# Block two's head units cut into five pieces, and every piece, search round and turn placed anew

## The reference

```
h = rms_norm(x, attn_norm_g);  proj = h @ w_in            # 1024 -> 3656 columns
mq, mk, mv, dq, dk, dv, sq, sk, sv, iq, ik, iw = split(proj)
qk(t) = rope(rms_norm(t per head of 64))                  # for mq, mk, dq, dk, sq, sk; iq and ik: rope alone
moba  = softmax(mq mk^T / 8, causal) mv                   # 4 heads
diff  = (softmax(q1 k1^T / 8) - lam * softmax(q2 k2^T / 8)) dv, then rms_norm per head   # 4 heads
score = sum over 8 heads of iw_h * relu(iq_h ik^T / 8);  keep the 64 highest keys of each query
dsa   = softmax(sq sk^T / 8 over the kept keys) sv        # 4 heads
x = x + concat(moba, diff, dsa) @ w_out
h2 = rms_norm(x, ffn_norm_g);  x = x + (silu(h2 @ w_gate) * (h2 @ w_up)) @ w_down
```

## Time and profile before

| | |
|---|---|
| median of three runs | 1726.27 us |
| profiled execution, its own time | 1728.09 us |
| its span, first to last instruction | 1726.3 us |
| mean granted TensorE clock | 0.973 |
| TensorE busy | 1611.4 us, 93% |
| VectorE busy | 1048.4 us, 61% |
| ScalarE busy | 768.1 us, 44% |
| DMA | 322.41 MB, mean 187 GB/s |

### The profile page before, as it was taken

How to read it: one execution, slowest core, us unless ns; L and a number is a source line. 1 busy time by engine, 2 the same in 40 slices (tenths; PEclk the granted TensorE clock), 3 DMA queues, 4 the chain that set the end, 5 groups by cost and what they waited for, 6 DMA issues and landing times.

```text
span 1726.3 us, 23453 instructions
## 1 busy us (share of the span) xinstructions
PE 1611.4 (93%) x9190; PEld 1315.3 (76%) x9190; DVE 1048.4 (61%) x1603; ACT 768.1 (44%) x1288; POOL 119.1 (7%) x130
## 2 busy tenths in 40 slices
PE   6999899999999989989999898689999997699998
PEld 3865676788888877578988676569998775589987
DVE  3627654753465356666765656648884657468873
ACT  3435523641354224545654465335453564344442
POOL 0210000000000001000000211000000201000000
PEclk8999999999999989999999999899999999899999
DMA  9448233873377224749986786136656674146653
GB/s 346 136 152 313 100 92 120 293 247 98 122 271 248 92 73 147 254 155 296 317 307 221 219 270 195 49 110 184 183 184 192 222 249 155 59 130 183 185 188 110
DMA packets 201005, 322.41 MB, mean 187 GB/s; under 512 B 14576, under 2 KB 100864, under 8 KB 200768
## 3 DMA queue, kind: packets, MB, share of 16 engines
q1 hardware_dynamic: 192992, 293.51, 53.2%
q0 software_dynamic: 7680, 27.34, 4.4%
q10 hardware_dynamic: 224, 0.07, 0.0%
HBM read 298.27 MB, written 22.61 MB: 186 GB/s over the span
## 4 chain that ended last, share of the span: by engine, by line
PE 83%; DVE 9%; DMA 2%; issue 2%; ACT 2%; POOL 1%; SPq 0%; DVEq 0%; ACTq 0%
PE bank L1925 50%; PE pair_bank L1925 20%; PE bank L1994 2%; DMA raw<-in_w_in 1%; PE bank L2212 1%; PE pair_bank L2230 1%; PE pair_bank L2184 1%; PE bank L2195 1%; DVE w_lo L1394 1%; DVE wide L1478 1%; PE bank L2244 1%; PE bank L2125 1%; PE bank L2450 1%; DMA raw<-in_w_ada 1%; DMA raw<-in_w_mlp 1%
## 5 line engine op out<-in xcount | busy, mean ns | idle before, releaser
L1394 DVE TENSOR_TENSOR w_lo<-raw,w_hi 128x1024 fp32r<-128x1024 f32 (+1 forms) x374 | 447.9, 1219 | 293.0 <-ACT w_hi L1059 291.1
L1059 ACT CAST w_hi<-raw 128x1024 fp32r<-128x1024 f32 (+2 forms) x416 | 428.1, 1043 | 393.1 <-PE bank L1925 293.8
L1925 PE MATMUL pair_bank<-act_hi,w_hi 128*128 128x256 f32 (+1 forms) x736 | 231.1, 314 | 11.6 <-DVE act_lo L1468 5.4
L1925 PE MATMUL pair_bank<-act_hi,w_lo 128*128 128x256 f32 (+1 forms) x736 | 227.7, 309 | 0.0
L1925 PE MATMUL pair_bank<-act_lo,w_hi 128*128 128x256 f32 (+1 forms) x736 | 227.5, 309 | 0.0
L1925 PE MATMUL bank<-w_hi,act_hi 128*128 128x512 f32 (+2 forms) x528 | 212.7, 403 | 11.0 <-ACT proj L1345 6.0
L1925 PE MATMUL bank<-w_hi,hid_lo 128*128 128x512 f32 x560 | 221.3, 395 | 0.0
L1925 PE MATMUL bank<-w_hi,hid_hi 128*128 128x512 f32 x560 | 221.3, 395 | 0.0
L1925 PE MATMUL bank<-w_lo,hid_hi 128*128 128x512 f32 x560 | 221.3, 395 | 0.0
L1925 PE MATMUL bank<-w_lo,act_hi 128*128 128x512 f32 (+2 forms) x528 | 204.8, 388 | 0.0
L1925 PE MATMUL bank<-w_hi,act_lo 128*128 128x512 f32 (+2 forms) x528 | 204.4, 387 | 0.0
(11 more groups left out here) (233 smaller groups left out, 2137.6 us busy)
## 6 DMA issues: line engine op xcount, KB each, us to landing
raw<-in_w_mlp SPq DMA_DIRECT2D x128, 512.0 KB, 4.4
raw<-in_w_in SPq DMA_DIRECT2D x112, 512.0 KB, 4.3
raw<-in_w_ada SPq DMA_DIRECT2D x96, 512.0 KB, 5.7
raw<-in_w_gate SPq DMA_DIRECT2D x44, 512.0 KB, 3.8
raw<-in_w_up SPq DMA_DIRECT2D x44, 512.0 KB, 3.8
raw<-in_w_down SPq DMA_DIRECT2D x44, 512.0 KB, 3.6
split_lo<-w_lo POOLq DMA_DIRECT2D x36, 512.0 KB, 4.9
w_lo<-split_lo SPq DMA_DIRECT2D x36, 512.0 KB, 4.8
```

The costliest lines, as they stand in the source:

```text
L1059: nc.scalar.copy(hi_of(i)[:, 0:w], raw[:, i % RAW, 0:w]).then_inc(hi_ready, 1)
L1394: nc.vector.tensor_tensor(w_lo[:, i % RAW, 0:w], raw[:, i % RAW, 0:w], hi_of(i)[:, 0:w].bitcast(F32), ALU.subtract).then_inc(lo_ready, 1)
L1925: ins = nc.tensor.matmul(o, a[x], b[y], start=first and i == 0, stop=True, skip_group_check=True)
```

## The change

The numbers of instructions and their sizes stay the same, but for a wait or two. What changes is the order:

1. `first` is cut into `var`, `cos`, `sin` and `sum`, so a unit has five pieces with `second`, each an entry of its own. `cos` has a wait of its own now, for the unit two before.
2. `FILL2` and `OUT2` are written anew. Scores begin at slot 13 instead of 11 and end beside slot 4 of out2 instead of slot 1; the search comes mostly in single rounds between other pieces. `lam` moves from slot 2 to slot 14. The table has an entry for slot 6 of out2's walk, which is empty.
3. At slot 3 of rows2 ScalarE does the drains of the first projection block (dq) ahead of its cast of a later slot, not behind it.
4. In `norm2` with m odd, `keep_busy` comes ahead of both `turn_row` calls and no longer between them.
5. `score` waits for the turned units at steps 0, 8 and 12 only.

The diff, with the table cut to three of its lines:

```diff
-            25: [("mix", 9), ("turn", 9), ("weigh", 10), ("score", 11), ("first", 10), ("search", 0, 2)],
+            26: [("weigh", 9), ("second", 9), ("search", 0, 1), ("drain", 6, 0), ("sum", 10), ("mix", 8), ("second", 10), ("turn", 9),
+                 ("score", 11)],
...
+            27: [("weigh", 10), ("search", 0, 1), ("weigh", 11), ("mix", 9), ("turn", 10), ("gather", 5), ("drain", 6, 1), ("search", 1, 1),
+                 ("search", 0, 2), ("mix", 10), ("search", 1, 1), ("mix", 11)],
...
             def rows2(self, l):          # Scalar
...
                 for step in range(29):
+                    if step == 3:
+                        self.extras2(FILL2, l, step)
                     self.step()
                     if step == 0:
                         for a in range(2):
                             self.norm_high(4 + 2 * l, 1, a)
-                    self.extras2(FILL2, l, step)
+                    if step != 3:
+                        self.extras2(FILL2, l, step)
...
+            def cosines(self, l, r):     # Vector
+                us = units2(l)
+                u = us[r]
+                if r > 1:
+                    self.e.wait_ge(rows_ready, n.at("rows_ready", us[r - 2]["key"]))
+                self.cosine_part(u, [("rows2", l, BLOCK2[u["block"]], t) for t in range(TT)])
...
             def norm2(self, m, l, which):    # Tensor
+                if m % 2:
+                    self.keep_busy()
                 self.turn_row(m, 0)
                 if m % 2:
-                    self.keep_busy()
                     self.turn_row(m, 1)
...
             def score(self, st, j):      # Tensor
                 e, key, w = self.e, st["key"], st["keys"] * P
-                u = units2(key[1])[(3, 3, 8, 10)[st["group"]]]
-                e.wait_ge(turned_out, n.at("turned_out", u["key"]))
+                if j in (0, 8, 12):
+                    for u in units2(key[1]):
+                        if u["block"] in {0: ("dq", "dk"), 8: ("mqk",), 12: ("sqk",)}[j]:
+                            e.wait_ge(turned_out, n.at("turned_out", u["key"]))
```

More of the change, by code:

```diff
@@ L330, in build @@
         FILL2 = {
[L331 to L352, removed]
@@ L353, in build @@
-            24: [("mix", 8), ("weigh", 9), ("score", 10), ("second", 9), ("search", 0, 2)],
-            25: [("mix", 9), ("turn", 9), ("weigh", 10), ("score", 11), ("first", 10), ("search", 0, 2)],
[L355 to L358, removed]
+            2: [("tables",)],
@@ new lines, in build @@
+            3: [("drain", 0, 0), ("var", 0), ("var", 1), ("cos", 0), ("sin", 0), ("cos", 1), ("sum", 0), ("sin", 1), ("drain", 0, 1)],
+            4: [("sum", 1), ("second", 0), ("second", 1)],
+            5: [("var", 3), ("cos", 3)],
+            6: [("sin", 3)],
+            7: [("var", 2), ("drain", 1, 0), ("drain", 1, 1), ("turn", 1)],
+            9: [("turn", 0)],
+            10: [("sum", 3), ("cos", 2), ("sin", 2), ("sum", 2)],
+            11: [("drain", 2, 0), ("second", 2), ("cos", 4), ("drain", 2, 1), ("turn", 2), ("second", 3), ("sin", 4)],
@@ new lines, in build @@
+            12: [("cos", 5), ("turn", 3)],
+            13: [("second", 4), ("score", 0)],
+            14: [("lam",), ("drain", 3, 0), ("turn", 4), ("score", 1), ("sin", 5), ("drain", 3, 1)],
+            15: [("weigh", 0), ("score", 2)],
+            16: [("weigh", 1), ("score", 3)],
+            17: [("second", 5), ("weigh", 2)],
+            18: [("drain", 4, 0), ("index_scale",), ("cos", 6), ("sin", 6), ("drain", 4, 1), ("second", 6), ("weigh", 3), ("turn", 6),
+                 ("var", 7), ("score", 4), ("var", 8), ("cos", 7), ("cos", 8)],
@@ new lines, in build @@
+            19: [("turn", 5), ("sin", 7), ("score", 5)],
+            20: [("sin", 8), ("logits", 0)],
+            21: [("weigh", 4), ("sum", 7), ("second", 7), ("gather", 0), ("sum", 8), ("second", 8), ("turn", 7), ("score", 6), ("logits", 1)],
+            22: [("weigh", 5), ("logits", 2), ("weigh", 6), ("gather", 1), ("search", 0, 1), ("drain", 5, 0), ("drain", 5, 1), ("search", 0, 1),
+                 ("gather", 2), ("turn", 8), ("score", 7)],
+            23: [("var", 10), ("cos", 10), ("var", 9), ("logits", 3), ("sin", 10), ("score", 8)],
@@ L359, in build @@
+            28: [("mix", 0), ("mix", 1), ("mix", 2), ("drain", 7, 0), ("mix", 3), ("mix", 4), ("search", 1, 1)],
         }
         OUT2 = {
[L361 to L364, removed]
+            0: [("search", 0, 1), ("mix", 5), ("mix", 6), ("mix", 7)],
@@ L365, in build @@
+            1: [("square", 0), ("drain", 7, 1), ("search", 1, 1), ("square", 1), ("score", 12)],
+            2: [("norm", 0), ("weigh", 12), ("norm", 1), ("search", 1, 2), ("turn_rows", 0), ("score", 13), ("search", 1, 2), ("turn_rows", 1)],
+            3: [("score", 14)],
+            4: [("mix", 12), ("weigh", 13), ("score", 15)],
+            5: [("weigh", 14), ("mix", 13), ("weigh", 15), ("mix", 14), ("mix", 15)],
         }
@@ L992, in out2 @@
             def out2(self, l):
-                for j in range(8):
+                for j in range(7):
                     self.extras2(OUT2, l, j)
```

81 lines of the change are left out of this document (57 added, 24 removed).

## The result

| | before | after |
|---|---|---|
| median | 1725.09 us (4 runs) | 1656.53 us (4 runs, 1654.81 to 1660.17) |
| ratio of times | | 0.9609, 95% interval 0.959 to 0.9629 |
| profiled execution's span | 1726.3 us | 1655.5 us |
| TensorE busy | 1611.4 us | 1590.9 us |
| mean granted clock | 0.973 | 0.986 |

The change made the kernel 68.6 us faster.

A forecast was written before the change was run, and what follows sets the result against it. TensorE, 83% of the chain of waits, was taken as the bound, losing time where it waits or is clocked low. 23.6 + 11.0 + 6.9 + 5.0 = 46.5 us off 1728.1 gave 1681.6 profiled, forecast 1680; range 1662 to 1705.

The forecast's parts named there:

- A: Rows2 slot 20 to out2 slot 5: TensorE's waits fall from 21.8 to 10.0 us a layer, gaining 23.6 for both.
- B: Half-clock work behind the attention waits: 7.3 us lost a layer, 1.8 kept as lost, gaining 11.0 for both layers.
- C: Drains at slot 3 of rows2 no longer await a DMA: 9.3 us gained, less 2.4 for late weights, net 6.9.
- D: Norm2 before up2: 28 transposes hide in the wait for `xn`, 3.5 us less 1.0 for clock a layer, 5.0 both.
- The walk: VectorE's new order stepped against TensorE's, rows2 slot 20 to out2 slot 5, with old durations: 5.6 us of waits a layer.
- the DMA takes over: Rival: slots 4 to 15 need 341 GB/s; a limit of 300 loses 10 us in all, giving 1690; chance 0.10.
- all of it: Rival: only 5.6 us of attention waits remain a layer, with no half clock: 1663 us at the median; chance 0.09.
- Half of it: Rival: the order still leaves 16 us of waits a layer and half the clock loss: 1695 at the median; chance 0.22.
- the slower rival: Late dsa scores 12 to 15 in out2 wait for the mask: 1762 us at full size, 1738 at half; chance 0.04.

The follow-up runs named there:

- the filled waits: The kernel before, with unread transposes issued on TensorE ahead of five of its waits in block two: 1715.7 us, ratio 0.9945.
- the late `weigh 11`: The changed kernel with the gather and four search rounds put ahead of `weigh 11`, so VectorE divides later for it: 1667.5 us, 0.9669 of before.
- the run with keep_busy first: The kernel before, with keep_busy ahead of both turn_row calls in norm2 (m odd) and nothing else: 1716.8 us, ratio 0.995.
- the drains' move alone: The kernel before, with ScalarE's drains of slot 3 ahead of its cast and nothing else: 1716.4 us, ratio 0.9947.
- the table alone: The changed kernel with the keep_busy and drains edits undone, leaving only the new table and cut units: 1668.2 us, 0.9662 of before.
- the rounds grouped: The changed kernel with single search rounds drawn together into rows of two, three and five: 1670.7 us, 0.9688 of before.

## Why the prediction was wrong

Of the 70.9 us of the stretch, these are the prediction's terms beside what the traces show:

| term | forecast | measured |
|---|---|---|
| A, waits | 23.6 | 39.3 |
| B, clock | 11.0 | 15.6 |
| C, drains | 6.9 | 8.3 |
| D, keep_busy | 5.0 | 7.6 |

Measured D is 2 × 3.8 us (11.0 less 7.2), 2.9 of it busy time. C is the wait of 5.6 and the slow slot of 1.8 in the first layer and the 1.9 of turns, less 1.0 for a new wait for a DMA at slot 6 of the first layer. A is the rest of the 50.5 us of idle time, B the rest of the 20.3 us of busy time.

**The step that failed is the surcharge in A.** The prediction walked the new order and found 5.6 us of waits a layer, and then added 4.4 us "for what it can't see". The walk itself was right to 0.7 us at every place: `weigh 11` 0.9 forecast and 0.8 found, `mix 4` 0.9 and 0.9, both `turn_rows` 2.1 and 1.4, the last chain 0.7 and 0.3, `weigh 8`, `weigh 13` and the exponentials 1.0 and none listed. That is 5.6 against 3.4. Beside them only 0.3 us is listed, a turn behind ScalarE's `relu_t`. What the walk could not see did not exist. Of the 15.7 us by which A was too small, the surcharge is 8.8 over both layers and the walk's excess over the 3.7 listed is 3.8; the last 3.1 are waits that the list of before names and the prediction left out of its 21.8. Two rows of the view of the earlier trace rows that it doesn't quote:

```profile
PE bank L2244 <- DVE probs L1769: 0.9, 3, 0.4
PE bank L2450 <- ACT pairs_t L1140: 0.7, 1, 0.7
```

The first layer has 1.0 and 0.7 us of them; after the change none is listed. Taking a value from the middle of the bounds looked prudent. It was a bias, and all the terms bent the same way.

**B** followed A. The allowance of 1.8 us a layer was for waits that follow each other at slot 2 of out2; one of 1.4 us is listed there, layer two has some 3 us at half clock behind it, and layer one none. Measured B (15.6) also lies above the bound of 14.6, which was worked out from 50 us of each layer alone. The mechanism stands, by the filled waits and by the late `weigh 11`: a wait was paid a second time at 0.4 us of busy time for each us of it in the change (20.3 to 50.5), and 0.6 in the run with one late `weigh` (5.1 to 8.5).

**C** lost 2.4 us to a DMA that was expected at slot 8. The trace has 1.0 us at slot 6 (the wait that ends at 986.5 us), and then 35 us in which TensorE is busy 34.96 while the DMAs move 343 GB/s. The rival "the DMA takes over" needed a limit of 300 GB/s, and falls. The Trainium skill, page "DMA: Bandwidth & Descriptors", section Specifications, gives some 358 GB/s for one core, by which the rival had to fall, and it did. As a limit the figure doesn't hold here: 383 GB/s in the 6.6 us from 979.9 lie above it, and the measurement decides.

**D** was charged 1.0 us a layer for a clock that didn't fall, and the way became 3.8 us shorter, not 3.5.

The rival "all of it" (1663) came nearest. It had the right mechanism and 0.09 of the chance, on the ground that no stretch of attention in the trace was that clean; but the trace was one of the old order, and says nothing of what a new one reaches. The range ended at it, since it was taken for the edge of what is possible, with the walk's own 5.6 us still in it. "Half of it" and the slower rival left no sign: the mask is in time at `score 12`, and out2's eight slots run at full clock but for one fall of some 3 us.

What stays open is how far the parts overlap: 73.9 us against 68.6 by medians, each good to 2 or 3 us, and 77.8 against 70.9 in the stretch. Of these 6.9 us, 2.7 are the chance wait of the run with keep_busy first. Some 1 us is a true overlap: the waits at slots 4 and 5 of the second layer (0.3 and 0.8) go with the drains' move alone and with the table alone. The rest isn't explained.

## What to carry to other kernels

Where an order is walked with durations from the trace, take its waits as they come out (here to 0.7 us at each place), and put doubt into the range and not into the sum: four small cautions of one sign (8.8, 3.6, 2.4 and 2.0 us) made up 16.8 of the 24.4 us by which the sum fell short of the stretch's 70.9. Count the waits of a stretch like this one at 1.4 to 1.6 times their length, for the clock behind them (1.40 over the whole change, 1.5 with the rounds grouped, 1.6 with one late `weigh`), and look for the piece that stands ahead of what TensorE needs next before cutting pieces smaller: the cuts gave nothing that could be measured, the places and the single rounds gave the table's gain. To judge an edit of a few us, measure the stretch it touches between two landmarks in the trace; the untouched middle repeated to 0.1 us in 13 of 14 traces (the fourteenth began at a lower clock), while the code ahead varied by 6 us from one execution to the next. Then split the stretch by layers and list the waits, since inside it chance is worth 2 to 3 us: one wait varied from 3.5 to 5.6 us, and a fall of the clock of some 3 us came behind a wait of 1.4 us in one layer and not in the other.

## What the runs showed of the hardware

The clock is held up by work that nobody reads: with 114 transposes a layer in place of the waits, the 50 us that had a granted clock of 0.80 had 1.00. It falls behind one wait of 5.3 us in a stretch that is otherwise full, at once and for about 7 us. Behind a wait of 1.4 us it fell in one layer of the changed kernel, for some 3 us, and not in the other. And one core's DMAs moved 343 GB/s for 35 us, at a share of 0.99, without TensorE losing more than 0.04 us.
